# A convolution whose turns run two tiles behind with its middle tap on ScalarE, and expert weights that come as whole gate or up matrices, in one kernel

## The chip, the cores and the metric

The kernel runs on one core of a Trainium2 chip, as one program. A core has five engines that run their own instruction streams and wait for one another by semaphores: TensorE (PE, matrix products; its weight loads are shown apart as PEld), VectorE (DVE), ScalarE (ACT), GpSimd (POOL) and SyncE (SP, which here only issues transfers), and 16 DMA engines that move data between memory and the core. The metric is the device time of one execution in microseconds, lower is better.

## What is computed

The reference chains two blocks of a transformer on 256 tokens of width 1024, each of two layers, all in 32-bit floats. Two places of it matter here. In each layer of the first block a mixture of 32 experts in 4 groups follows the attention: each token goes to one group and to two experts of it.

```python
for g in range(N_GROUPS):
    h = jax.nn.silu(jnp.einsum('td,edf->tef', t, w_gate[g])) * jnp.einsum('td,edf->tef', t, w_up[g])
    y = y + jnp.einsum('tef,efd->td', h * gate[:, g, :, None], w_down[g])
```

Gate and up matrices are 1024 x 256 for each expert, down matrices 256 x 1024. In the second layer of the second block a projection of width 4096 (2048 for x, 1024 each for B and C) goes through a depthwise convolution over the sequence, on 256 tokens of the sequence and 256 of a context:

```python
xbc = jax.nn.silu(dwconv(xbc, conv_w, conv_b))          # 5 taps per channel
xs, bm, cm = jnp.split(xbc, [SSD_DI, SSD_DI + SSD_GN], axis=-1)
```

## The kernel before

**Experts.** Tokens are sorted to experts, 32 places for each; four experts make a quad, whose four products lie side by side in four groups of 32 columns of TensorE. There are eight main quads a layer (all 32 experts) and four overflow quads (8 to 11) for tokens beyond 32, whose experts are chosen at run time. Each quad needs three pieces of weights of 4 MB (f32): k = 0 and k = 1 for gate and up, k = 2 for down. `STEPS_E` sets the order of the quads. The pieces go through a ring of four slots (WQ0, WQ1, W, and a fourth made of a part of XA and of EX); main pieces are issued by SyncE in the order (q, k) at line 480, each as soon as its slot is free (`await_used`), overflow pieces as conditional transfers on ScalarE's queue (`overflow_load`, line 1067). `plan_ring` counts what each slot's semaphore has to reach. Before, pieces 0 and 1 are halves of the rows of K: piece 0 holds K rows 0 to 3 of each partition's eight of both gate and up, piece 1 the other four, and a matmul of `gate_up` (line 731) multiplies 32 columns of tokens with 512 columns, gate beside up. Each such matmul of 32-bit floats shows as two records in the trace: a part has 4 rows of K x 4 experts x 2 = 32. A piece's source is 4 KB in a row for each partition and expert. A down piece has 8 KB in a row. After gate and up VectorE and ScalarE make silu(gate) x up, TensorE turns it (line 554) and `down` multiplies it (line 768).

**Convolution.** The 4096 channels make 32 tiles of 128 channels: m = 0 to 15 (x) and 16 to 23 (B) with 512 columns (sequence and context), called wide here, 24 to 31 (C) with 256, called narrow. For a tile, ScalarE makes the high part PHI of the weights (`conv_high`, line 2784), VectorE the low part WLO (`conv_low`, line 3296), both two tiles ahead; TensorE does 24 matmuls (line 2201) into a bank; ScalarE copies the bank into PRE (`conv_taken`, helper line 2611), which has two padding columns at each side; VectorE adds up five taps into ACC (line 3384 the first, line 3386 the other four); ScalarE applies silu and the bias into XD (`conv_out`, lines 2817 to 2822; ARENA is the memory that holds PRE, ACC and XD); TensorE turns XD to have tokens on partitions ("xt", line 2206), for tiles 0 to 23; and ScalarE copies the turned tile (`conv_turned`). TensorE's order is written out by hand: the matmuls of tile m ("sc", m), then the turn of tile m-1. The eight banks are handed out by the same order. Between the first tiles ScalarE has other work with tables of its own to load (`dt_logs` at m = 2).

## Time and profile before

| | |
|---|---|
| median of 3 runs | 2192.19 us (2192.07 to 2196.28) |
| the profiled execution | 2194.47 us, its span 2192.7 us |
| mean granted clock of TensorE | 0.961 |
| busy: PE, DVE, ACT, POOL | 1977.7, 1256.6, 743.2, 168.1 us |
| moved by DMA | 441.03 MB in 152322 packets, 143856 of them under 8 KB |

The span is from the first to the last instruction of one profiled execution; the device time has a little more around it. The granted clock is the share of full speed that the chip's throttle gave TensorE; its two levels are 1.2 and 2.4 GHz, so that 1.00 in a window is 2.4 GHz throughout and 0.50 is 1.2 GHz. The expert stages lie at 255 to 470 us (layer 0) and 700 to 942 us (layer 1), the convolution at 1605 to 1806 us.

### The profile page before, as it was taken

To read this page: it belongs to the slowest core of one execution; us is meant where nothing else is said; L and a number is where in the kernel's file an instruction comes from. 1 tells how busy PE (TensorE), PEld (TensorE's weight loads), DVE (VectorE), ACT (ScalarE), POOL (GpSimd) and SP (SyncE) were. 2 spreads that over 40 slices of the span, in tenths; PEclk is the share of its full clock that TensorE was granted. 3 is DMA by queue.
4 is the path that set the end of the run, shared out by engine and by line. 5 is a ranking of instruction groups with operands and counts; after the bars stand their busy time and mean duration, and the time that the engine had idled before them with its cause. 6 is when DMAs were issued, how large, how long until landed. Compare 5 with 4: busy or idle time off the path is not lost.

```text
span 2192.7 us, 31068 instructions
## 1 busy us (share of the span) xinstructions
PE 1977.7 (90%) x12070; PEld 1445.9 (66%) x12070; DVE 1256.6 (57%) x2223; ACT 743.2 (34%) x1338; POOL 168.1 (8%) x156
## 2 busy tenths in 40 slices
PE   6989888879899788969998999999979989998997
PEld 4776433337785333337887778888867777777996
DVE  3374522135474212257375776666766887877676
ACT  3363311114552111144233311122164446743332
POOL 2001100010002000034413000000100000000000
PEclk9999999989999999979999999999989999999999
DMA  7479899965699999932212323322222334234552
GB/s 222 168 285 348 322 411 413 413 249 192 224 363 325 362 399 413 413 117 77 77 39 82 130 96 116 105 88 83 80 69 97 118 133 173 77 116 173 192 192 96
DMA packets 152322, 441.03 MB, mean 201 GB/s; under 512 B 10640, under 2 KB 13120, under 8 KB 143856
## 3 DMA queue, kind: packets, MB, share of 16 engines
q1 hardware_dynamic: 143232, 413.77, 50.6%
q0 software_dynamic: 8224, 22.13, 3.3%
q10 hardware_dynamic: 720, 3.15, 0.4%
q8 instruction: 97, 1.59, 0.3%
q14 instruction: 49, 0.40, 0.1%
HBM read 535.31 MB, written 1.21 MB: 245 GB/s over the span
## 4 chain that ended last, share of the span: by engine, by line
PE 39%; DVE 7%; ACT 4%; DVEq 3%; issue 1%; ACTq 0%; DMA 0%; SPq 0%
PE bank L2201 21%; PE bank L2294 12%; PE bank L2345 4%; PE bank L2573 2%; ACT ARENA L2873 1%; DVE ARENA L3386 1%; PE bank L2206 1%; DVEq L3345 1%; DVEq L2971 0%; ACT UT L2634 0%; DVE ARENA L3404 0%; DVEq L3388 0%; ACT ARENA L2611 0%; DVEq L3406 0%; DVE MB L3333 0%
## 5 line engine op out<-in xcount | busy, mean ns | idle before, releaser
L2647 ACT ACTIVATE WPH<-W 128x1024 fp32r<-128x1024 f32 x128 | 135.6, 1064 | 381.1 <-PE bank L2201 200.6
L2201 PE MATMUL bank<-UH,WPH 128*128 128x512 f32 (+1 forms) x512 | 174.6, 341 | 7.2 <-DVE UL L2979 3.1
L2201 PE MATMUL bank<-UL,WPH 128*128 128x512 f32 (+1 forms) x512 | 173.7, 339 | 0.0
L2201 PE MATMUL bank<-UH,WPL 128*128 128x512 f32 (+1 forms) x512 | 173.4, 339 | 0.0
L3017 DVE TENSOR_TENSOR WPL<-W,WPH 128x1024 fp32r<-128x1024 f32 x128 | 153.5, 1220 | 18.6 <-ACT WPH L2647 18.6
L2294 PE MATMUL bank<-WPH,MHH 128*128 128x512 f32 x384 | 149.5, 389 | 0.0
L2294 PE MATMUL bank<-WPL,MHH 128*128 128x512 f32 x384 | 149.5, 389 | 0.0
L2294 PE MATMUL bank<-WPH,MHL 128*128 128x512 f32 x384 | 149.4, 389 | 0.0
L1501 DVE TENSOR_TENSOR H<-SG,bank 128x256 f32<-128x256 f32 x24 | 10.1, 421 | 211.5 <-ACT SG L1073 211.5
L2201 PEld LDWEIGHTS bank<-UH,WPH 128*128 128x128 f32 x512 | 98.4, 192 | 20.0 <-issue 3.8
L2201 PE MATMUL bank<-ARENA 128*128 128x64 f32 (+4 forms) x528 | 102.1, 350 | 6.3 <-issue 2.8
L2201 PEld LDWEIGHTS bank<-UL,WPH 128*128 128x128 f32 x512 | 98.4, 192 | 10.3
L2201 PEld LDWEIGHTS bank<-UH,WPL 128*128 128x128 f32 x512 | 98.4, 192 | 10.2
L2201 PE MATMUL bank<-XHI,PHI 128*128 128x512 f32 (+2 forms) x264 | 101.4, 384 | 4.0 <-DVE XLO L2979 2.4
L2201 PE MATMUL bank<-XHI,WLO 128*128 128x512 f32 (+2 forms) x264 | 98.4, 373 | 0.0
L2201 PE MATMUL bank<-XLO,PHI 128*128 128x512 f32 (+2 forms) x264 | 98.0, 371 | 0.0
L2611 ACT ACTIVATE ARENA<-bank 128x512 f32<-128x512 f32 (+3 forms) x108 | 58.1, 559 | 116.3 <-PE bank L2201 79.2
L731 PE MATMUL bank<-WQ,XG 128*32 128x512 f32 x704 | 83.8, 620 | 14.6 <-DMA WQ<-in_expert_w_up 10.3
L2201 PEld LDWEIGHTS bank<-ARENA 128*128 128x128 f32 (+1 forms) x528 | 77.0, 197 | 26.6 <-issue 22.1
L561 PE MATMUL bank<-W,XT 128*128 128x512 f32 x192 | 88.4, 620 | 6.6 <-ACT XT L912 4.0
L3386 DVE SCALAR_TENSOR_TENSOR ARENA<-ARENA 128x512 f32<-128x512 f32 (+1 forms) x128 | 87.7, 685 | 10.3 <-issue 0.9
L1510 DVE SCALAR_TENSOR_TENSOR EXPERT_ROWS_LOW<-bank,GSLOT,EXPERT_ROWS_HIGH 128x512 fp32r<-128x512 f32 x48 | 34.6, 748 | 94.9 <-ACT EXPERT_ROWS_HIGH L1086 94.9
(482 smaller groups left out, 4412.1 us busy)
## 6 DMA issues: line engine op xcount, KB each, us to landing
W<-in_ffn_w SPq DMA_DIRECT2D x64, 1024.0 KB, 6.6
W<-in_ada_w SPq DMA_DIRECT2D x32, 1024.0 KB, 7.4
WQ<-in_expert_w_gate SPq DMA_DIRECT2D x16, 2048.0 KB
WQ<-in_expert_w_up SPq DMA_DIRECT2D x16, 2048.0 KB
WQ<-in_expert_w_down SPq DMA_DIRECT2D x16, 2048.0 KB
W<-in_w_in SPq DMA_DIRECT2D x24, 1024.0 KB, 7.7
WQ<-in_expert_w_down ACTq DMA_DIRECT2D x24, 1024.0 KB
W<-in_ssd_w_in SPq DMA_DIRECT2D x24, 1024.0 KB, 6.4
```

Of the source, the lines that this page charges most:

```text
L561: last = nc.tensor.matmul(bank[r.bank(key)][:, 0:n], lhs[k], rhs[k], start=(k == 0), stop=(k == len(lhs) - 1))
L731: last = nc.tensor.matmul(bank[r.bank(key)][32 * g:32 * g + 32, :], xg[:, 4 * part + k, col:col + 32], half_of(slot, g, g + 1)[:, 0, :, k, ...
L1510: r.read_done(nc.vector.scalar_tensor_tensor(YL[:, sl], bank[r.bank(key)][:, :], GSLOT[:, q:q + 1], YH[:, sl].bitcast(F32), ALU.mult, ALU. ...
L2201: return nc.tensor.matmul(bank[r.bank(key)][0:rows, cols[0]:cols[1]], lhs, rhs, start=start, stop=stop)
L2206: return nc.tensor.transpose(bank[r.bank(key)][0:m, j * P:j * P + k], src, ident[0:k, 0:k])
L2294: last = nc.tensor.matmul(bank[r.bank(key)][:, :], a, x[:, k, :], start=first and k == 0 and z == 0, stop=last_block and kp == 1 and k == ...
L2345: last = nc.tensor.matmul(bank[r.bank(key)][:, :], x[:, kk, tok], a[:, k, :], start=kp == 0 and k == 0 and z == 0, stop=kp == 3 and k == 1 ...
L2573: last = nc.tensor.matmul(bank[r.bank(key)][:, :], y[:, kk % 2, c0:c0 + P], w[:, k, :], start=kk == 0 and z == 0, stop=kk == 15 and z == 2 ...
L2611: r.read_done(nc.scalar.activation(dst, src, func, **kw), key)
L2647: nc.scalar.activation(piece_view(WPH, q), piece_src(i, q), ACT.Copy).then_inc(hi_done, 1)
L3017: nc.vector.tensor_tensor(piece_view(WPL, q), piece_src(i, q), piece_view(WPH, q).bitcast(F32), ALU.subtract).then_inc(lo_done, 1)
L3386: last = nc.vector.scalar_tensor_tensor(acc, src, CW[:, m, k:k + 1], acc, ALU.mult, ALU.add)
```

## The change

Two parts. In the experts, piece 0 of a quad is now the whole gate matrix of four experts and piece 1 the whole up matrix, 8 KB in a row for each partition and expert; a piece is two transfers of two experts each (one and three in the fourth slot). A matmul multiplies with 256 columns, and there are twice as many. In the convolution, the turn stands two tiles behind the matmuls (`TURN_LAG`), XD has three buffers, the third of which is YI, and ScalarE writes the middle tap straight from the bank into ACC, scaled by a column of weights, so that VectorE has four taps to add and no first one.

```diff
--- before.py
+++ after.py
@@ -55,10 +55,9 @@
     fills = [[] for _ in range(RING)]
     for i in range(3 * MQ):
         q, k = divmod(i, 3)
-        split = 2 if i % RING == RING - 1 else 1
-        fills[i % RING].append(((q, k), 16 * (2 if k == 2 else 2 * split)))
+        fills[i % RING].append(((q, k), 16 * 2))
         if q in OVERFLOW_OF:
-            fills[i % RING].append(((OVERFLOW_OF[q], k), 16 * (4 if k == 2 else 8)))
+            fills[i % RING].append(((OVERFLOW_OF[q], k), 16 * 4))
     at = {}
     for slot, made in enumerate(fills):
         total = 0
@@ -307,8 +306,8 @@
                 return whole[slot][:, g0:g1]
             return first_of_last if g0 == 0 else EX[:, g0 - 1:g1 - 1]
 
-        def half_of(slot, g0, g1):
-            return ring(slot, g0, g1).rearrange("p g (u k f) -> p g u k f", u=2, k=4)
+        def whole_of(slot, g0, g1):
+            return ring(slot, g0, g1).rearrange("p g (k f) -> p g k f", k=KT)
 
         def down_of(slot, g0, g1):
             return ring(slot, g0, g1).rearrange("p g (f n) -> p g f n", f=2)
@@ -382,20 +381,14 @@
         up_w = io["expert_w_up"].rearrange("l g e (p k) f -> (l g e) p k f", p=P)
         down_w = io["expert_w_down"].rearrange("l g e (p k) n -> (l g e) p k n", p=P)
 
-        def piece(slot, what, part, first, g0, g1):
-
-            if what == 2:
-                return down_w[bass.ds(first, g1 - g0)].rearrange("e p k n -> p e k n"), down_of(slot, g0, g1)
-            src = (gate_w, up_w)[part][bass.ds(first, g1 - g0), :, 4 * what:4 * what + 4, :]
-            return src.rearrange("e p k f -> p e k f"), half_of(slot, g0, g1)[:, :, part]
-
-        def parts_of(slot, k):
-
-            if slot == RING - 1:
-                cuts = [(0, 1), (1, 4)]
-            else:
-                cuts = [(0, 2), (2, 4)] if k == 2 else [(0, 4)]
-            return [(part, g0, g1) for part in range(1 if k == 2 else 2) for g0, g1 in cuts]
+        def piece(slot, what, first, g0, g1):
+
+            src = (gate_w, up_w, down_w)[what][bass.ds(first, g1 - g0)].rearrange("e p k n -> p e k n")
+            return src, (down_of if what == 2 else whole_of)(slot, g0, g1)
+
+        def cuts_of(slot):
+
+            return [(0, 1), (1, 4)] if slot == RING - 1 else [(0, 2), (2, 4)]
 
         def await_used(eng, l, key, before):
 
@@ -475,8 +468,8 @@
                     if i == 3:
                         r.filled(sp, ("rout", 1), l)
                     await_used(sp, l, (q, k), True)
-                    for part, g0, g1 in parts_of(i % RING, k):
-                        src, dst = piece(i % RING, k, part, l * NEXP + (4 * q + g0), g0, g1)
+                    for g0, g1 in cuts_of(i % RING):
+                        src, dst = piece(i % RING, k, l * NEXP + (4 * q + g0), g0, g1)
                         sp.dma_start(dst, src).then_inc(landed[i % RING], 16)
             sp.wait_ge(used[2], DEPTH * RING_USES[2] + 1)
             for n, key in enumerate(list(after)[0:SLOTS]):
@@ -725,11 +718,11 @@
                         slot = weights_landed(l, part, q)
                         if part == 0:
                             r.claim(pe, key, l)
-                        for k in range(4):
+                        for k in range(KT):
                             for g in range(4):
                                 col = (q % 2) * P + 32 * g
-                                last = nc.tensor.matmul(bank[r.bank(key)][32 * g:32 * g + 32, :], xg[:, 4 * part + k, col:col + 32],
-                                                        half_of(slot, g, g + 1)[:, 0, :, k, :], start=(part == 0 and k == 0), stop=(part == 1 and k == 3))
+                                last = nc.tensor.matmul(bank[r.bank(key)][32 * g:32 * g + 32, part * EH:(part + 1) * EH], xg[:, k, col:col + 32],
+                                                        whole_of(slot, g, g + 1)[:, 0, k, :], start=(k == 0), stop=(k == KT - 1))
                         if part == 0:
                             last.then_inc(used[slot], 1)
                             if between is not None and q == a:
@@ -1061,10 +1054,9 @@
 
                     slot = PIECE_AT[(q, k)][0]
                     await_used(act, l, (q, k), True)
-                    for part in range(1 if k == 2 else 2):
-                        for g in range(4):
-                            src, dst = piece(slot, k, part, l * NEXP + ids[g], g, g + 1)
-                            nc.scalar.dma_start(dst, src, cond=on[g]).then_inc(landed[slot], 16)
+                    for g in range(4):
+                        src, dst = piece(slot, k, l * NEXP + ids[g], g, g + 1)
+                        nc.scalar.dma_start(dst, src, cond=on[g]).then_inc(landed[slot], 16)
 
                 def silu(q):
 
@@ -1642,6 +1634,7 @@
 NB = 8
 PIECES = 4
 CUM_AT = 8
+TURN_LAG = 2
 TINY = 1e-37
 X_LN = (4, 8, 10, 12)
 SQ_LN = (2, 6, 9, 11)
@@ -1721,13 +1714,12 @@
         r.plan(("uT", "m1", s, j), b)
     keys = [("dt",), ("dtT",)]
     conv = []
-    for m in range(NX + 2 * SG_ + 1):
+    for m in range(NX + 2 * SG_):
         if m == CUM_AT:
             conv += [("cum",), ("cd",)]
-        if m < NX + 2 * SG_:
-            conv.append(("sc", m))
-        if 1 <= m <= NX + SG_:
-            conv.append(("xt", m - 1))
+        conv.append(("sc", m))
+        if TURN_LAG <= m < NX + SG_ + TURN_LAG:
+            conv.append(("xt", m - TURN_LAG))
     keys += conv
     for n, k in enumerate(keys):
         r.plan(k, {("sc", NX + 2 * SG_ - 2): 6, ("sc", NX + 2 * SG_ - 1): 7}.get(k, n % 8))
@@ -1932,7 +1924,7 @@
         o = 18432
         PRE = A_[:, o:o + 1040].rearrange("p (b s n) -> p b s n", b=2, s=2)
         ACC = A_[:, o + 1040:o + 2064].rearrange("p (b s n) -> p b s n", b=2, s=2)
-        XD = A_[:, o + 2064:o + 3088].rearrange("p (b n) -> p b n", b=2)
+        XD = [A_[:, o + 2064:o + 2576], A_[:, o + 2576:o + 3088], YI[:].rearrange("p t n -> p (t n)")]
         CW = A_[:, o + 3088:o + 3280].rearrange("p (m k) -> p m k", k=6)
         SUMS = A_[:, o + 4096:o + 5120].rearrange("p (z j n) -> p z j n", z=2, j=2)
         CVR = A_[0:6, 8192:12288]
@@ -2476,20 +2468,19 @@
                         last = mm(key, (z * SEQ, (z + 1) * SEQ), DA[:, jt, z * 32:z * 32 + 32], SUMS[:, z, jt, :], jt == 0, jt == 1, rows=32)
                 r.fill_done(last, key)
 
-            for m in range(NX + 2 * SG_ + 1):
+            for m in range(NX + 2 * SG_):
                 if m == CUM_AT:
                     sums()
-                if m < NX + 2 * SG_:
-                    key = ("sc", m)
...
-                    r.fill_done(last, key)
+                key = ("sc", m)
...
+                r.fill_done(last, key)
                 if m == 0:
                     key = ("dtT",)
                     r.read(pe, ("dt",))
@@ -2497,12 +2488,13 @@
                     for t in range(4):
                         last = turn(key, t, DTL[:, t * P:(t + 1) * P])
                     r.fill_done(last, key)
-                if 1 <= m <= NX + SG_:
-                    key = ("xt", m - 1)
-                    pe.wait_ge(xd_rdy, m)
+                if TURN_LAG <= m < NX + SG_ + TURN_LAG:
+                    q = m - TURN_LAG
+                    key = ("xt", q)
+                    pe.wait_ge(xd_rdy, q + 1)
                     r.claim(pe, key)
-                    for t in range(4) if m - 1 < NX else range(2, 4):
-                        last = turn(key, t, XD[:, (m - 1) % 2, t * P:(t + 1) * P])
+                    for t in range(4) if q < NX else range(2, 4):
+                        last = turn(key, t, XD[q % 3][:, t * P:(t + 1) * P])
                     r.fill_done(last, key)
 
             def group_pre(g):
@@ -2809,15 +2801,15 @@
             def conv_out(q):
 
                 act.wait_ge(acc_rdy, q + 1)
-                if 2 <= q < NX + SG_:
-                    r.filled(act, ("xt", q - 2))
+                if 3 <= q < NX + SG_:
+                    r.filled(act, ("xt", q - 3))
                 acc = ACC[:, q % 2]
                 bias = CW[:, q, 5:6]
                 if q < NX:
-                    nc.scalar.activation(XD[:, q % 2, :].rearrange("p (s n) -> p s n", s=2), acc, ACT.Silu, bias=bias).then_inc(xd_rdy, 1)
+                    nc.scalar.activation(XD[q % 3].rearrange("p (s n) -> p s n", s=2), acc, ACT.Silu, bias=bias).then_inc(xd_rdy, 1)
                 elif q < NX + SG_:
                     nc.scalar.activation(BDL[:, q - NX, :], acc[:, 0, :], ACT.Silu, bias=bias)
-                    nc.scalar.activation(XD[:, q % 2, SEQ:2 * SEQ], acc[:, 1, :], ACT.Silu, bias=bias).then_inc(xd_rdy, 1)
+                    nc.scalar.activation(XD[q % 3][:, SEQ:2 * SEQ], acc[:, 1, :], ACT.Silu, bias=bias).then_inc(xd_rdy, 1)
                 else:
                     nc.scalar.activation(CDL[:, q - NX - SG_, :], acc[:, 0, :], ACT.Silu, bias=bias).then_inc(xd_rdy, 1)
 
@@ -2827,7 +2819,12 @@
                 ns = 2 if m < NX + SG_ else 1
                 if m >= 2:
                     act.wait_ge(acc_rdy, m - 1)
-                copy(key, PRE[:, m % 2, 0:ns, 2:2 + SEQ], bank[r.bank(key)][:, 0:ns * SEQ].rearrange("p (s n) -> p s n", s=ns))
+                src = bank[r.bank(key)][:, 0:ns * SEQ].rearrange("p (s n) -> p s n", s=ns)
+                r.filled(act, key)
+                nc.scalar.activation(PRE[:, m % 2, 0:ns, 2:2 + SEQ], src, ACT.Copy)
+                if m == 0:
+                    r.read(act, ("cw",))
+                r.read_done(nc.scalar.activation(ACC[:, m % 2, 0:ns], src, ACT.Copy, scale=CW[:, m, SCONV // 2:SCONV // 2 + 1]), key)
 
             def conv_turned(q):
 
@@ -2851,8 +2848,8 @@
                 if m >= 1:
                     conv_out(m - 1)
                 conv_taken(m)
-                if 1 <= m <= NX + SG_:
-                    conv_turned(m - 1)
+                if TURN_LAG <= m < NX + SG_ + TURN_LAG:
+                    conv_turned(m - TURN_LAG)
 
             def segments(g):
 
@@ -3379,13 +3376,11 @@
                     v.wait_ge(xd_rdy, m - 1)
                 acc = ACC[:, m % 2, 0:ns]
                 for k in range(SCONV):
-                    src = PRE[:, m % 2, 0:ns, k:k + SEQ]
-                    if k == 0:
-                        last = nc.vector.tensor_scalar(acc, src, CW[:, m, 0:1], None, ALU.mult)
-                    else:
+                    if k != SCONV // 2:
+                        src = PRE[:, m % 2, 0:ns, k:k + SEQ]
                         last = nc.vector.scalar_tensor_tensor(acc, src, CW[:, m, k:k + 1], acc, ALU.mult, ALU.add)
-                    if k < SCONV - 1:
-                        v.drain()
+                        if k < SCONV - 1:
+                            v.drain()
                 last.then_inc(acc_rdy, 1)
 
             for t in range(2):
```

On SyncE, the first pieces of a layer (after the layer's other loads); 128x4x1024 is partitions x experts x elements in a row. Before:

```order
L480 DMA WQ<-in_expert_w_gate 128x4x1024
L480 DMA WQ<-in_expert_w_up 128x4x1024
L480 DMA WQ<-in_expert_w_gate 128x4x1024
L480 DMA WQ<-in_expert_w_up 128x4x1024
L480 DMA W<-in_expert_w_down 128x2x2048 x2
L480 DMA XA<-in_expert_w_gate 128x1024
L480 DMA EX<-in_expert_w_gate 128x3x1024
L480 DMA XA<-in_expert_w_up 128x1024
L480 DMA EX<-in_expert_w_up 128x3x1024
```

and now:

```order
L473 DMA WQ<-in_expert_w_gate 128x2x2048 x2
L473 DMA WQ<-in_expert_w_up 128x2x2048 x2
L473 DMA W<-in_expert_w_down 128x2x2048 x2
L473 DMA XA<-in_expert_w_gate 128x2048
L473 DMA EX<-in_expert_w_gate 128x3x2048
L473 DMA WQ<-in_expert_w_up 128x2x2048 x2
L473 DMA WQ<-in_expert_w_down 128x2x2048 x2
```

The gate matrix comes first as one piece, and the up matrix as a piece of its own; rows are 2048 elements long, as those of down were, and the fourth slot's piece is two transfers instead of four.

On TensorE, the convolution's first tiles: L2201 are a tile's matmuls (L2193 in the changed kernel), of which the first stands here, and L2206 (L2198) is the turn of a tile, which waits for silu by the semaphore b_conv_out. The wait b_mixer_weights_low is for VectorE's low part. Before:

```order
L2201 MATMUL bank<-XHI,PHI 128x512 [waits b_empty3,b_mixer_weights_low]
...
L2206 MATMUL bank<-ident,ARENA 128x128 [waits b_empty4,b_conv_out]
...
L2201 MATMUL bank<-XHI,PHI 128x512 [waits b_empty5,b_mixer_weights_low]
...
L2206 MATMUL bank<-ident,ARENA 128x128 [waits b_empty6,b_conv_out]
...
L2201 MATMUL bank<-XHI,PHI 128x512 [waits b_empty7,b_mixer_weights_low]
```

and now:

```order
L2193 MATMUL bank<-XHI,PHI 128x512 [waits b_empty3,b_mixer_weights_low]
...
L2193 MATMUL bank<-XHI,PHI 128x512 [waits b_empty4,b_mixer_weights_low]
...
L2198 MATMUL bank<-ident,ARENA 128x128 [waits b_empty5,b_conv_out]
...
L2193 MATMUL bank<-XHI,PHI 128x512 [waits b_empty6,b_mixer_weights_low]
...
L2198 MATMUL bank<-ident,ARENA 128x128 [waits b_empty7,b_conv_out]
...
L2193 MATMUL bank<-XHI,PHI 128x512 [waits b_empty0,b_mixer_weights_low]
...
L2198 MATMUL bank<-ident,YI 128x128 [waits b_empty1,b_conv_out]
```

Two tiles' matmuls now stand ahead of the first turn, and between the silu of a tile and its turn there is always one more tile.

On ScalarE, one wide tile in the middle: L2784 (L2776) the high part for two tiles ahead, L2817 (L2809) silu, L2611 or L2824 the copy of the bank into PRE, L2611 (L2603) of 128x4x128 the copy of the turned tile; b_conv_sum is VectorE's sum of the taps. Before:

```order
L2784 ACTIVATE PHI<-W 128x1024 [waits b_full5]
L2817 ACTIVATE ARENA<-ARENA 128x512 [waits b_full4,b_conv_sum]
L2611 ACTIVATE ARENA<-bank 128x2x256 [waits b_full7,b_conv_sum]
L2611 ACTIVATE ARENA<-bank 128x4x128 [waits b_full0]
L2784 ACTIVATE PHI<-W 128x1024 [waits b_full7]
```

and now:

```order
L2776 ACTIVATE PHI<-W 128x1024 [waits b_full4]
L2809 ACTIVATE YI<-ARENA 128x512 [waits b_conv_sum]
L2824 ACTIVATE ARENA<-bank 128x2x256 [waits b_full6,b_conv_sum]
L2827 ACTIVATE ARENA<-bank,ARENA 128x512
L2603 ACTIVATE ARENA<-bank 128x4x128 [waits b_full7]
L2776 ACTIVATE PHI<-W 128x1024 [waits b_full6]
```

The row of L2827 is added in each tile: the middle tap, from the same bank as the copy above it. On VectorE line 3384, one instruction in each tile, is gone.

## Rows read from the trace of the kernel before

**Rows 1.** Page, part 1: busy time, share of the span, instructions.
```profile
PE 1977.7 (90%) x12070; PEld 1445.9 (66%) x12070; DVE 1256.6 (57%) x2223; ACT 743.2 (34%) x1338; POOL 168.1 (8%) x156
```

**Rows 2.** Windows: us, busy (x) of five engines, PEclk, DMA share, GB/s.
```profile
core 0: us, PE busy (x) PEld busy (x) DVE busy (x) ACT busy (x) POOL busy (x), PEclk, DMA share, GB/s
342.00:353.00 11.00, 9.65 (x88) 2.98 (x83) 4.09 (x9) 2.41 (x5) 0.00 (x0) 1.00 1.02 408
905.00:918.00 13.00, 11.38 (x104) 3.70 (x100) 3.54 (x8) 2.77 (x6) 0.00 (x0) 1.00 1.03 410
391.00:396.00 5.00, 4.72 (x32) 1.15 (x32) 0.00 (x0) 0.00 (x0) 0.00 (x0) 0.68 1.01 421
835.00:839.00 4.00, 4.00 (x28) 1.84 (x24) 0.00 (x0) 0.00 (x0) 0.00 (x0) 1.00 1.02 424
258.00:457.00 199.00, 172.16 (x1346) 75.04 (x1342) 50.40 (x103) 29.42 (x56) 0.00 (x0) 0.97 1.02 413
750.00:760.00 10.00, 9.44 (x76) 2.63 (x72) 2.03 (x5) 1.15 (x3) 0.00 (x0) 0.87 0.94 360
...
463.40:469.40 6.00, 5.97 (x32) 1.61 (x32) 0.75 (x1) 0.69 (x1) 0.00 (x0) 0.51 1.05 387
935.60:941.00 5.40, 5.34 (x32) 1.56 (x32) 0.75 (x1) 0.69 (x1) 0.00 (x0) 0.68 0.81 305
```

**Rows 3.** Timeline, TensorE and its weight loads, expert stages: start, us, [idle before].
```profile
163.81 1.95 PE L656 MATMUL bank<-W,cond 128*32 128x128 f32 x64
...
340.60 3.64 PE L731 MATMUL bank<-W,XG 128*32 128x512 f32 x32
...
340.60 0.16 PEld L731 LDWEIGHTS bank<-W,XG 128*32 128x32 f32 x4 [0.27 <-issue]
...
463.43 1.03 PE L768 MATMUL bank<-XA,H 128*32 128x512 f32 x1 [4.14 <-DMA EX<-in_expert_w_down]
...
935.63 0.59 PE L768 MATMUL bank<-XA,H 128*32 128x512 f32 x1 [2.90 <-DMA EX<-in_expert_w_down]
```

**Rows 4.** Idle time before turns (line 2206); two of them in the timeline.
```profile
  ACT ARENA L2820: 5.0, 3
  ACT ARENA L2817: 4.8, 3
...
1634.07 1.11 PE L2206 MATMUL bank<-ident,ARENA 128*128 128x128 f32 x4 [3.15 <-ACT ARENA L2817]
...
1778.01 0.44 PE L2206 MATMUL bank<-ident,ARENA 128*128 128x128 f32 x2 [2.46 <-ACT ARENA L2820]
```

**Rows 5.** Windows of the convolution, columns as in rows 2.
```profile
1634.80:1641.00 6.20, 6.20 (x18) 4.89 (x17) 5.45 (x10) 2.27 (x3) 0.00 (x0) 0.58 0.00 0
...
1643.50:1679.50 36.00, 36.00 (x172) 28.39 (x171) 23.15 (x30) 13.42 (x20) 0.00 (x0) 0.95 0.34 118
```

**Rows 6.** Timeline of the convolution, VectorE and ScalarE, wide then narrow tiles.
```profile
1632.01 1.23 DVE L3296 TENSOR_TENSOR WLO<-W,PHI 128x1024 fp32r<-128x1024 f32 x1 [3.06 <-ACT PHI L2784]
...
1656.30 3.23 DVE L3386 SCALAR_TENSOR_TENSOR ARENA<-ARENA 128x512 f32<-128x512 f32 x4
...
1785.67 0.51 ACT L2822 ACTIVATE ARENA<-ARENA 128x256 f32<-128x256 f32 x1 [1.91 <-DVE ARENA L3386]
...
1789.32 0.51 ACT L2822 ACTIVATE ARENA<-ARENA 128x256 f32<-128x256 f32 x1 [1.92 <-DVE ARENA L3386]
1789.73 0.37 ACT L2611 ACTIVATE ARENA<-bank 128x256 f32<-128x256 f32 x1
...
1787.11 2.18 DVE L3386 SCALAR_TENSOR_TENSOR ARENA<-ARENA 128x256 f32<-128x256 f32 x4
1789.20 1.22 DVE L3296 TENSOR_TENSOR WLO<-W,PHI 128x1024 fp32r<-128x1024 f32 x1
```

**Rows 7.** Groups of ScalarE from 1160 to 1812 us: xcount, busy, mean ns.
```profile
L2784 ACT ACTIVATE PHI<-W 128x1024 fp32r<-128x1024 f32 x32 | 33.7, 1057 | 0.0
...
L2817 ACT ACTIVATE ARENA<-ARENA 128x512 f32<-128x512 f32 x16 | 11.6, 724 | 31.9 <-DVE ARENA L3386 31.8
...
L2726 ACT ACTIVATE XHO<-bank,ARENA 128x512 fp32r<-128x512 f32 x8 | 4.8, 694 | 0.0
```

More of the change, by code:

```diff
@@ L2477, in sums @@
                 r.fill_done(last, key)
[L2479 removed]
+            for m in range(NX + 2 * SG_):
                 if m == CUM_AT:
                     sums()
[L2482 to L2492 removed]
+                key = ("sc", m)
+                pe.wait_ge(conv_lo, m + 1)
+                hi = PHI[:, m % 3]
+                lo = WLO[:, number[("sc", m // 4)] % SLOTS, :, (m % 4) * P:(m % 4 + 1) * P]
+                width = 512 if m < NX + SG_ else SEQ
+                r.claim(pe, key)
+                for k in range(KT):
+                    for z, (a, x) in enumerate(((hi, XHI), (hi, XLO), (lo, XHI))):
+                        last = mm(key, (0, width), a[:, k, :], x[:, k, 0:width], k == 0 and z == 0, k == KT - 1 and z == 2)
+                r.fill_done(last, key)
                 if m == 0:
```

8 lines of the change are left out of this document (removed).

## The prediction

> **What bounds the kernel now.** I read the page first: TensorE is busy for 90% of the span [rows 1], so what shortens the kernel is TensorE's idle time and its time at a lower clock. Both parts of the change lie in stretches where TensorE stands idle, and those I read by windows and by the timeline.
>
> In the expert stages two things run side by side. From 258 to 457 us TensorE is busy 172.16 of 199 us, while the DMA engines are full and move 413 GB/s [rows 2]. So the weights' arrival sets the pace, and TensorE has 199 − 172 = 27 us to spare in layer 0. That it is the arrival that ends last is seen at each stage's end: the last down-product waits 4.14 us for its weights in layer 0 and 2.90 us in layer 1 [rows 3]. In layer 1 before about 795 us the queue is not full (360 GB/s from 750 to 760 us [rows 2]): the next piece waits there for a free slot, and a faster transfer brings nothing.
>
> In the convolution TensorE sets the pace of wide tiles: 36.0 of 36 us busy for six tiles, so 6.0 us a tile [rows 5]. But its turn of tile m-1 stands right behind the matmuls of tile m and waits for ScalarE's silu of tile m-1: 4.8 us in three waits and 5.0 us in three [rows 4]. The longest is 3.15 us, and behind it the granted clock is 0.58 for 6.2 us [rows 5], that is, part of these at 1.2 GHz.
>
> **The expert part.** The bytes stay. A gate or up piece comes in 8 KB rows instead of 4 KB rows. Stretches in which only gate and up pieces land run at 408 to 410 GB/s (four windows), and stretches in which only down pieces land, which have 8 KB rows already, at 421 to 424 GB/s (four windows); in all of them the DMA share is full [rows 2]. A piece is 4 experts × 1024 × 256 × 4 bytes = 4.194 MB: 10.25 us at 409, 9.93 us at 422.5, so −0.33 us for each piece that lands in a full queue. Layer 0 has 13 of them after 255 us (8 main quads give 16, three come earlier): −4.2. Layer 1 has about 8.5 after 795 us: −2.8. Together −7.0. A bound from the other side is nothing at all (the slower rate of gate and up pieces is then due to something that goes with them other than the row length, as the matmuls that run beside them); the upper bound is all sixteen pieces of each layer plus four overflow pieces' share, −8.8.
>
> The Trainium skill, "DMA: Bandwidth & Descriptors", section "Why small descriptors are slow (HBM only)", has the overhead of a packet fixed at a few cycles beside its beats, by which I estimate from its figures that going from 4 KB to 8 KB would bring about 1.1%, or 0.12 us a piece and 2.5 us in all. The rows have 3.3% between the two kinds, three times as much; I go by the rows.
>
> TensorE pays for that: a part is 64 records of 256 columns instead of 32 of 512. Columns are the same, so the question is what a record costs beside its columns. 32 records of 512 columns on 32-column weights take 3.64 us, 64 records of 128 columns with the same weights' shape take 1.95 us [rows 3]: 107 and 29 ns a record from start to start of the next work, and on the straight line between them a 256-column record takes 55 ns, 64 of them 3.54 us where 32 wide ones took 3.42. That is +0.1 us a part, 24 parts a layer, +2.7 us a layer, under 27 us of spare time [rows 2]: it lies beside the transfers. Its cover is the last wait; it shrinks from 4.14 and 2.90 us to some 2 and 0.5 us (the transfers gain on TensorE there, and the records cost it a little), and stays above nothing. I take +0.3 for the last quad.
>
> Behind those last waits the clock is down: the last down-product has 0.51 and 0.68 granted, and 32 records that take 3.64 us at full clock take 5.97 and 5.34 us [rows 2, 3]. That is 2.3 + 1.7 = 4.0 us. If the shorter wait leaves the clock up, most comes back; a drop followed waits of 2.90 us and more here, and the 2 and 0.5 us that I expect are shorter. I take −3, bounds 0 and −4.
>
> The issue side: SyncE issues a piece as two DMAs of two experts (in slot 3, two instead of four), ScalarE's queue four conditional ones instead of eight for an overflow piece. Nothing is behind these that TensorE waits for, and the queue always has a piece pending in the full stretches: nothing taken. Expert part: −7.0 + 0.3 − 3 = −9.7 (from 0 to −12.8).
>
> **The convolution part.** With the turn two tiles behind, silu of tile m-2 has to be done when the matmuls of tile m are, a whole tile (6.0 us) later than needed before. The longest wait of the turns is 3.15 us, so each has cover of over 2.8 us. The waits that go: 4.8 + 5.0 us less the last, 2.46 us [rows 4], which stands in front of the narrow tiles, where TensorE is not the one that ends last: −7.3. With them goes the low clock after the 3.15 us wait: 6.2 × (1 − 0.58) = −2.6. What could be late next: VectorE's low part, which for one tile waits 3.06 us for ScalarE's high part [rows 6], behind three table loads (bound: that tile's wait stays whole, −3.15 and −2.6 are lost, −5 for the conv part remain); and ScalarE, which gets one more eviction in each tile. A scaled eviction of 512 columns takes 0.69 us, the high part 1.06, silu 0.72 [rows 7]. With all three evictions at that price ScalarE's tile is 3 × 0.69 + 1.06 + 0.72 = 3.9 of 6.0 us: covered by TensorE. VectorE loses its first tap and keeps four of 3.23 us together and the low part of 1.22, 4.5 of 6.0 us [rows 6].
>
> In the eight narrow tiles VectorE and ScalarE set the pace, 3.65 us a tile (silu at 1785.67 and 1789.32 [rows 6]). There the chain closes over ScalarE afterwards: four taps take 2.1 us from start to VectorE's next work (1787.11 to 1789.20), silu starts 0.12 later, the eviction 0.41 after that; it takes 0.37, some 0.3 from start to start, and the second one between 0.37 and 0.69 [rows 6, 7], of which I take 0.45, nearer to the row of the same width; 0.1 to the first tap. 2.1 + 0.12 + 0.41 + 0.3 + 0.45 + 0.1 = 3.45 us or so. 7 × −0.2 = −1.3, and at the end the last tile's second eviction stands ahead of a table load, +0.4: −0.9. With the upper price of the eviction the narrow tiles give nothing.
> Conv part: −7.3 − 2.6 − 0.9 = −10.8 (−5 to −12 where it works).
>
> **Sum.** −9.7 − 10.8 = −20.5 on the profiled execution's 2194.5 us (span 2192.7 and 1.8 around it) = 2174.0; the median of the runs shown is 2.3 lower, 2192.2, which gives 2171.7. As the clock's and the rate's terms lose more on one side than they can win on the other, I say 2173.
>
> **The rivals.**
> *Slower: weight loads that are no longer hidden.* A quartet of loads takes 0.16 us on TensorE's load side [rows 3] and today lies behind 0.43 us of matmuls. With 256 columns the quartets are 16 a part instead of 8, each of 0.22 us. If the loads came in series, a part would take 16 × (0.22 + 0.16) = 6.1 instead of 3.6 us, +2.4, ×24 = +58 us of TensorE time a layer against 27 spare: +31 a layer, +62 in all, with conv −10.8: about 2243. It decides from 27 / 24 = 1.1 us a part on. Against it: 64 records of a quarter of the width took 1.95 us together [rows 3], no 16 × 0.16 on top. 5%. The Trainium skill, "TensorE: Matmul & The Clock Gate", section "The mechanism" (of the part on packing small matmuls), has a weight load overlap the matmuls in flight only where the row group differs; all four here use all 128 rows, so by it this rival would hold. The row of 64 quarter-width records disagrees.
> *The rate does not follow the row length.* Then the conv part alone: 2192.2 − 10.8 = 2181.4. For it: gate and up pieces land beside the matmuls of their own slots, down pieces often in stretches of less engine work. 12%.
> *The wait only moves (conv).* The low part or ScalarE is late in the turn's place: expert part alone, about 2183. 10%.
> *Neither:* 2192. 6%.
> Both as forecast: 67%, with a range of its own of 2166 to 2178.
>
> **How the numbers follow.** A measurement of this kernel tells about 0.2% (4.4 us) from no change. Faster: 67 + 12 + 10 = 89%. Same: 6%, slower: 5%. The range of 8 in 10 reaches down to 2164 (all upper bounds) and up to 2186, past the two cases in which one part works.
>
> **What would show it.** In the profile after: windows with gate and up pieces alone at over 418 GB/s, packets under 8 KB down by at least 33,000 (32 main pieces of 4.194 MB in 4 KB); 64 records of a gate_up part within 3.7 us; last waits under 2.9 us and the granted clock of the last down-product near 1; no wait of a turn for silu over 0.3 us; granted clock 1 behind tile 2; narrow tiles at 3.45 us. The prediction is wrong if a part's 64 records take over 4.7 us, if windows stay at 409, or if VectorE's low part ends TensorE's waits in the convolution.

## The result and the profile after

| kernel | median, us | runs | ratio to the kernel before, 95% |
|---|---|---|---|
| before, beside the changed kernel | 2189.56 (2182.11 to 2196.28) | 12 | |
| changed | 2176.29 (2170.18 to 2184.53) | 12 | 0.9941 [0.9925, 0.9957] |
| changed, once more (x_again) | 2174.24 | 6 | 0.9930 [0.9905, 0.9955] |

The change makes the kernel 13 us (0.6%) faster; 2173 was forecast, from 2192.2. The profiled executions lie further apart, spans of 2192.7 and 2174.6 us, 18 us. Executions of one kernel spread over 14 us here, and the profiled one of before is 5 us above the median of its 12 runs; so a profile's difference of a few microseconds is read below only where other profiles repeat it. Four executions, three of the kernel before and one of t_tap, took 2562 to 8280 us and are left out of the medians below.

The page after: the span, busy time, and the packets.

```profile
span 2174.6 us, 33931 instructions
PE 1973.4 (91%) x13606; PEld 1502.3 (69%) x13606; DVE 1242.7 (57%) x2191; ACT 759.0 (35%) x1370; POOL 168.4 (8%) x156
DMA packets 135404, 441.21 MB, mean 203 GB/s; under 512 B 10352, under 2 KB 12832, under 8 KB 110288
```

TensorE has 1536 more records [rows 1], the narrower matmuls of the experts; packets under 8 KB fell by 33,568, of which 32,768 are the 32 main pieces' (4.194 MB each in rows of 4 KB). The bytes are the same within 0.2 MB.

Windows after, in the columns of [rows 2]: layer 0's full stretch, and the last down-products of both layers.

```profile
258.00:457.00 199.00, 173.81 (x2047) 100.87 (x2048) 50.87 (x105) 29.52 (x57) 0.00 (x0) 0.97 1.01 418
...
459.70:463.40 3.70, 3.64 (x32) 1.13 (x32) 0.75 (x1) 0.69 (x1) 0.00 (x0) 1.00 1.03 350
929.20:934.40 5.20, 5.20 (x32) 1.27 (x32) 0.75 (x1) 0.69 (x1) 0.00 (x0) 0.69 0.84 314
```

The queue moves 418 GB/s over 199 us where it moved 413 [rows 2]. The last down-product of layer 0 runs at the full clock (3.64 us, before 5.97 in its window), that of layer 1 at 0.69 as before (0.68). TensorE's timeline at these places:

```profile
452.27 3.66 PE L724 MATMUL bank<-W,XG 128*32 128x256 f32 x64
...
459.74 0.59 PE L761 MATMUL bank<-XA,H 128*32 128x512 f32 x1 [2.41 <-DMA EX<-in_expert_w_down]
...
929.20 1.03 PE L761 MATMUL bank<-XA,H 128*32 128x512 f32 x1 [3.25 <-DMA EX<-in_expert_w_down]
```

A part of 64 records takes 3.66 us (32 wide ones took 3.64 [rows 3]). The last wait shrank from 4.14 to 2.41 us in layer 0; in layer 1 it did not, 3.25 after 2.90.

The convolution's turns, by the view of line 2198 from 1603 to 1765 us: what TensorE waited for ahead of them, and how often.

```profile
its engine sat idle before it (us, times) until:
  issue: 0.4, 1
```

No turn waits for silu any more, where [rows 4] has 4.8 + 5.0 us. The narrow tiles, ScalarE and VectorE in the timeline:

```profile
1776.90 0.51 ACT L2814 ACTIVATE ARENA<-ARENA 128x256 f32<-128x256 f32 x1 [1.28 <-DVE ARENA L3381]
1777.31 0.37 ACT L2824 ACTIVATE ARENA<-bank 128x256 f32<-128x256 f32 x1
1777.58 0.47 ACT L2827 ACTIVATE ARENA<-bank,ARENA 128x256 f32<-128x256 f32 x1
...
1780.28 0.51 ACT L2814 ACTIVATE ARENA<-ARENA 128x256 f32<-128x256 f32 x1 [1.28 <-DVE ARENA L3381]
...
1776.78 1.22 DVE L3293 TENSOR_TENSOR WLO<-W,PHI 128x1024 fp32r<-128x1024 f32 x1
1778.08 2.17 DVE L3381 SCALAR_TENSOR_TENSOR ARENA<-ARENA 128x256 f32<-128x256 f32 x4
```

A narrow tile takes 3.38 us (1776.90 to 1780.28), before 3.65 [rows 6]; 3.45 was forecast. The second eviction takes 0.47 us and ends at 1778.05, the low part at 1778.00: the two now bound the start of the taps together.

### The profile page after: what moved, and what is told of

It reads as the page before. It is cut to its first block, busy times and chain, and to the rows that moved or that the text cites. A ratio compares the mean times of both kernels' runs of the same rounds, so it can differ in the third digit from the quotient of the medians.

```text
span 2174.6 us, 33931 instructions
## 1 busy us (share of the span) xinstructions
PE 1973.4 (91%) x13606; PEld 1502.3 (69%) x13606; DVE 1242.7 (57%) x2191; ACT 759.0 (35%) x1370; POOL 168.4 (8%) x156
## 3 DMA queue, kind: packets, MB, share of 16 engines
q10 hardware_dynamic: 432, 3.15, 0.3%
## 4 chain that ended last, share of the span: by engine, by line
PE 41%; DVE 7%; ACT 4%; DVEq 3%; issue 1%; ACTq 0%; DMA 0%; SPq 0%
PE bank L2193 23%; PE bank L2286 12%; PE bank L2337 4%; PE bank L2565 2%; ACT ARENA L2870 1%; DVE ARENA L3381 1%; PE bank L2198 1%; DVEq L3342 1%; DVE ARENA L3399 0%; ACT UT L2626 0%; DVEq L3401 0%; ACTq L2629 0%; DVE MB L3330 0%; DMA W<-in_ffn_w 0%; DVE XA L2969 0%
## 5 line engine op out<-in xcount | busy, mean ns | idle before, releaser
L2193 PE MATMUL bank<-UH,WPH 128*128 128x512 f32 (+1 forms) x512 | 174.3, 340 | 8.0 <-DVE UL L2976 3.8
L2193 PE MATMUL bank<-UL,WPH 128*128 128x512 f32 (+1 forms) x512 | 173.2, 338 | 0.0
L2193 PE MATMUL bank<-UH,WPL 128*128 128x512 f32 (+1 forms) x512 | 173.1, 338 | 0.0
L1493 DVE TENSOR_TENSOR H<-SG,bank 128x256 f32<-128x256 f32 x24 | 10.1, 421 | 206.1 <-ACT SG L1065 206.1
L2193 PEld LDWEIGHTS bank<-UH,WPH 128*128 128x128 f32 x512 | 98.2, 192 | 20.5 <-issue 4.5
L2193 PE MATMUL bank<-ARENA 128*128 128x64 f32 (+4 forms) x528 | 103.0, 352 | 6.3 <-issue 2.8
L2193 PEld LDWEIGHTS bank<-UL,WPH 128*128 128x128 f32 x512 | 98.3, 192 | 10.3
L2193 PEld LDWEIGHTS bank<-UH,WPL 128*128 128x128 f32 x512 | 98.1, 192 | 10.2
L2193 PE MATMUL bank<-XHI,PHI 128*128 128x512 f32 (+2 forms) x264 | 100.1, 379 | 4.7 <-DVE XLO L2976 2.4
L2193 PE MATMUL bank<-XHI,WLO 128*128 128x512 f32 (+2 forms) x264 | 97.6, 370 | 0.0
L2193 PE MATMUL bank<-XLO,PHI 128*128 128x512 f32 (+2 forms) x264 | 97.2, 368 | 0.0
L2193 PEld LDWEIGHTS bank<-ARENA 128*128 128x128 f32 (+1 forms) x528 | 77.8, 198 | 26.5 <-issue 21.2
L724 PE MATMUL bank<-WQ,XG 128*32 128x256 f32 x1408 | 83.3, 391 | 11.2 <-DMA WQ<-in_expert_w_up 6.6
L1065 ACT ACTIVATE SG<-bank 128x256 f32<-128x256 f32 x24 | 9.2, 384 | 228.0 <-PE bank L724 125.3
```

Source lines behind the costliest of these rows:

```text
L724: last = nc.tensor.matmul(bank[r.bank(key)][32 * g:32 * g + 32, part * EH:(part + 1) * EH], xg[:, k, col:col + 32], whole_of(slot, g, g + ...
L2193: return nc.tensor.matmul(bank[r.bank(key)][0:rows, cols[0]:cols[1]], lhs, rhs, start=start, stop=stop)
```

## The experiments

Times are medians; the kernel before had 2190.9 us beside the four kernels whose names begin with x, 2190.6 beside those with t and 2190.3 beside those with u. Stretches are read from the timelines: layer 0 and layer 1 from the first gate_up matmul to the end of the last down matmul, the convolution from its first matmul to the first of the next stage.

| profile of | rows, order | layer 0 | layer 1 | its end to the convolution | convolution |
|---|---|---|---|---|---|
| before | 4 KB, old | 218.5 | 228.0 | 663.6 | 201.4 |
| x_conv | 4 KB, old | 217.7 | 224.9 | 663.6 | 186.3 |
| u_conv | 4 KB, old | 218.3 | 226.3 | 663.8 | 188.0 |
| u_cols | 4 KB, old, 256 columns | 218.8 | 227.6 | 661.9 | 186.3 |
| x_rows | 4 KB, new | 218.8 | 229.1 | 663.2 | 186.3 |
| u_rows | 4 KB, new | 219.7 | 228.6 | 663.7 | 188.0 |
| changed | 8 KB, new | 212.9 | 226.0 | 666.8 | 188.0 |
| x_again | 8 KB, new | 212.8 | 223.9 | 663.1 | 187.9 |
| x_exp | 8 KB, new | 214.6 | 225.8 | 666.6 | 197.0 |
| t_lag | 8 KB, new | 212.8 | 226.2 | 666.7 | 189.8 |
| t_tap | 8 KB, new | 215.4 | 225.4 | 666.7 | 194.5 |
| t_busy | 8 KB, new | 214.8 | 223.8 | 665.4 | 188.0 |
| t_cols | 4 KB, old, 256 columns | 218.8 | 240.5 | 662.9 | 188.0 |

**x_conv and u_conv: the convolution part alone.** The kernel before with the changes from TURN_LAG on.

```diff
+TURN_LAG = 2
-        XD = A_[:, o + 2064:o + 3088].rearrange("p (b n) -> p b n", b=2)
+        XD = [A_[:, o + 2064:o + 2576], A_[:, o + 2576:o + 3088], YI[:].rearrange("p t n -> p (t n)")]
...
+                r.read_done(nc.scalar.activation(ACC[:, m % 2, 0:ns], src, ACT.Copy, scale=CW[:, m, SCONV // 2:SCONV // 2 + 1]), key)
```

> The convolution part alone, the experts as before. If the parts are independent: the stretch from the convolution's first matmul to the first matmul of the next stage, 201.4 us before and 188.0 us with both parts, is 188 here too; no turn waits; the narrow tiles are 3.38 us apart; the time is 11 to 13 us below the kernel before. If part of the gain in that stretch is given back later (a lower clock in the stages behind it), the stretch is 188 us but the time is only 6 to 8 us lower. The expert stages (first gate_up matmul to last down matmul, 218.5 us in layer 0 and 228.0 us in layer 1 before) stay within 1.5 us of that; a larger difference is the run-to-run spread of TensorE's clock in the same code.

> The convolution part alone once more, beside the other two: 2176 us as before if 6 runs were enough to know it; if it comes out at 2179 to 2182, the expert part was worth more than the 0 to 2 us that the first comparison gave it.

2176.11 us (0.9934 [0.9912, 0.9955]) and, again, 2176.88 us (0.9935 [0.9909, 0.9960]): 13 to 15 us below the kernel before, beyond the 11 to 13 that were expected. The stretch is 186.3 and 188.0 us, no turn waits. Nothing of it is given back. So the convolution part alone has nearly the whole gain of the change. The two values of the stretch come back in the table, 186.3 or 188.0, and the granted clock tells them apart: ten microseconds from 55 us behind the first matmul, in x_conv and then in u_conv,

```profile
1660.43:1670.43 10.00, 10.00 (x60) 7.97 (x59) 4.14 (x5) 3.16 (x5) 0.00 (x0) 1.00 0.60 210
```

```profile
1658.98:1668.98 10.00, 10.00 (x52) 7.15 (x51) 4.14 (x5) 3.17 (x5) 0.00 (x0) 0.83 0.60 210
```

0.17 of 10 us are the 1.7 us.

**x_exp: the expert part alone.** The kernel before with the changes ahead of TURN_LAG.

```diff
+        def whole_of(slot, g0, g1):
+            return ring(slot, g0, g1).rearrange("p g (k f) -> p g k f", k=KT)
...
+                        for k in range(KT):
```

> The expert part alone, the convolution as before. By the profile of both parts together layer 0 took 212.9 us instead of 218.5 and layer 1 226.0 instead of 228.0: 5.7 + 2.0 = 7.6 us less, and so 5 to 8 us below the kernel before. The rival: what layer 0 gained at its end (2.8 us of full clock in the last down-product) was that one execution's luck, and only the rate remains, 4 to 5 us. The convolution's stretch should be 201 us as before, with the same waits of turns (about 7.3 us before the narrow tiles, the longest 3.2 us).

2187.08 us, ratio 0.9991 [0.9975, 1.0008]: the medians differ by 3.8 us, the interval holds no change at all. Layer 0 came down as expected (214.6 us), layer 1 to 225.8, which is where the three kernels with the old experts lie (224.9 to 228.0). The part is worth less than the two stretches say. It is also a second profile of the convolution of before, whose stretch was expected at 201 us and is 197.0, and there it tells against a term of the forecast. The turn that waits longest, and a window behind it (to be held against [rows 4, 5]):

```profile
1638.62 0.66 PE L2198 MATMUL bank<-ident,ARENA 128*128 128x128 f32 x4 [3.17 <-ACT ARENA L2809]
...
1639.40:1645.40 6.00, 6.00 (x30) 4.90 (x29) 5.42 (x10) 2.65 (x4) 0.00 (x0) 1.00 0.00 0
```

The wait is there as it was, 3.17 us, and the clock behind it is 1.00, not 0.58. The drop in the profile of before was not a fixed price of that wait; t_tap below has a wait of 3.36 us at the same place, and 1.00 in the six microseconds behind it.

**x_again: the changed kernel once more.**

> The changed kernel once more, beside the others on one chip: 11 to 15 us below the kernel before. If the two parts add up, its gain is the sum of the gains of the two parts alone within 3 us; if one hides behind the other or they share clock, it is less by more than that. Its profile shows which of the stages repeat: layer 0 at 213 and layer 1 at 226 us, the convolution at 188 us; a stage that comes out over 2 us away shows how far one execution's clock reaches.

2174.24 us, 0.9930 [0.9905, 0.9955]. The stretches of layer 0 and of the convolution repeat within 0.1 us; layer 1 and what lies behind it come out 2 and 4 us shorter. Gains of the parts alone are 14.7 and 3.8 us, 18.5 together, beside 16.6 here and 13.3 in the first set: the parts add up as far as these sets can tell, with a 3.8 that is not clear of no change by itself.

**x_rows and u_rows: the changed kernel with 4 KB rows.** Only the transfers differ from the changed kernel: halves of K, into the same places.

```diff
-            src = (gate_w, up_w, down_w)[what][bass.ds(first, g1 - g0)].rearrange("e p k n -> p e k n")
-            return src, (down_of if what == 2 else whole_of)(slot, g0, g1)
+            src = (gate_w, up_w)[what][bass.ds(first, g1 - g0), :, 4 * part:4 * part + 4, :]
+            return src.rearrange("e p k f -> p e k f"), whole_of(slot, g0, g1)[:, :, 4 * part:4 * part + 4]
```

> The changed kernel, but each gate or up piece is fetched as two halves of K in 4 KB rows into the same places; pieces, matmuls and their order stay as in the changed kernel. If the row length makes the rate: stretches with gate and up pieces alone fall from 419 to 424 back to 408 to 410 GB/s, the last waits for the down weights grow again to about 4 and 3 us, and the time is 5 to 8 us above the changed kernel. If the rate was due to the order of the pieces or the narrower matmuls, it stays at about 420 and the time within 2 us of the changed kernel.

> The changed kernel with 4 KB rows once more: 2181 us if the row length is worth the 5 to 7 us that the first comparison gave it; within 2 us of the convolution part alone if the difference between them was the spread of the clock between sets of runs.

2181.39 us (0.9960 [0.9946, 0.9974]) and 2183.67 us (0.9967 [0.9952, 0.9981]): 5 to 9 us above the two medians of the changed kernel, neither of which was taken beside u_rows. Layer 0 is back at 218.8 and 219.7 us, and so is the rate. The same window as above, in x_rows, and the last wait:

```profile
258.00:457.00 199.00, 173.18 (x2032) 100.94 (x2034) 50.09 (x103) 29.06 (x55) 0.00 (x0) 0.97 1.02 413
...
463.27 1.03 PE L768 MATMUL bank<-XA,H 128*32 128x512 f32 x1 [3.86 <-DMA EX<-in_expert_w_down]
```

With matmuls and order of the changed kernel the queue moves 413 GB/s again: the rate is the row length's. From the ends of the packets in the trace (packets of 4 KB and more of SyncE's queue counted off in pieces of 4.194 MB, the last sixteen pieces of layer 0), a gate or up piece takes 10.29 us in the kernel before, 10.30 in x_rows, 10.03 in the changed kernel and 10.04 in x_exp. The down pieces between them, with 8 KB rows in all four, take 9.9 to 10.1 us there.

But both sets stand 5 to 7 us above the convolution part alone too, which has the same 4 KB rows. So the new order of the pieces with its narrower matmuls goes with about as much more time as the longer rows bring. That was not foreseen. Part of it can be the clock, whose mean over the executions is 0.9640 and 0.9628 in x_conv and u_conv, 0.9622 and 0.9613 in x_rows and u_rows: by an estimate from these, clock difference times span, at most 3.9 and 3.3 us, which leaves 1.4 and 3.5 us.

**t_cols and u_cols: narrower matmuls alone.** The convolution part with the pieces of before, each matmul made as two; in t_cols gate and up each start their sums in a bank, in u_cols a bank starts once.

```diff
+                        for u in range(2):
...
-                                                        half_of(slot, g, g + 1)[:, 0, :, k, :], start=(part == 0 and k == 0), stop=(part == 1 and k == 3))
+                                                            half_of(slot, g, g + 1)[:, 0, u, k, :], start=(part == 0 and u == 0 and k == 0), stop=(part == 1 and u == 1 and k == 3),
```

> The convolution part with the experts' pieces of before (halves of K of gate and up in 4 KB rows), but each matmul of 512 columns made as one of 256 for gate and one of 256 for up. If narrower matmuls cost what 64 records in 3.66 us instead of 32 in 3.64 say, it is within 2 us of the convolution part alone (2176 us). If they cost more than that in the program (weight loads, instruction fetch), it is 3 us or more above it, which would explain why the changed kernel with 4 KB rows is 5 us above the convolution part alone.

2196.03 us (1.0025 [1.0010, 1.0041]), 20 us above the convolution part. The sums of gate and up are not the reference's in this kernel, so layer 1 routes its tokens otherwise (ScalarE's queue moves 6.29 MB of overflow pieces, in the other kernels 3.15) and takes 240.5 us, 14 more than with the old experts. Only layer 0 can be read: 218.8 us, as with wide matmuls.

> Again the convolution part with the experts' pieces of before, each matmul of 512 columns made as two of 256, now with sums that start once for a bank, so that layer 1 routes as in the reference and the whole time can be read. If the narrower matmuls are what the changed order costs in the experts: about 2181 us, as the changed kernel with 4 KB rows (2181.4), 5 us above the convolution part alone. If narrower matmuls cost nothing beside the transfers: 2176 us, and the 5 us lie in the order of the pieces or in the spread of the clock between sets of runs.

2179.54 us (0.9952 [0.9934, 0.9971]): between the two expectations, 2.7 us above the convolution part measured beside it and 4.1 below u_rows; the intervals of it and of the convolution part overlap. Its mean granted clock, 0.9632, is not below that of u_conv (0.9628). The first two parts of layer 1 together, in u_conv and then in u_cols:

```profile
713.92 7.07 PE L731 MATMUL bank<-WQ,XG 128*32 128x512 f32 x64 [0.94 <-issue]
```

```profile
715.70 7.11 PE L732 MATMUL bank<-WQ,XG 128*32 128x256 f32 x128 [0.94 <-issue]
```

0.02 us a part. If the narrower matmuls cost 2.7 us, it is not in the records themselves.

**t_lag and t_tap: the halves of the convolution part.** In t_tap the turn stands one tile behind (the first edit below); in t_lag VectorE adds five taps again (the second, in part).

```diff
-TURN_LAG = 2
+TURN_LAG = 1
```

```diff
-                    if k != SCONV // 2:
+                    if k == 0:
+                        last = nc.vector.tensor_scalar(acc, src, CW[:, m, 0:1], None, ALU.mult)
+                    else:
```

> The changed kernel, but VectorE adds all five taps again and ScalarE writes no tap: of the convolution part only the turn two tiles behind is left. If the lag alone removes the waits of the turns: no turn waits, the wide tiles take as long as in the changed kernel (about 156 us from the first matmul of the convolution to the first narrow tile), and the narrow tiles go back from 3.38 to 3.65 us, so that the stretch is some 2 us longer than the 188 us of the changed kernel and the time 1 to 3 us above it. If the tap is what matters, turns still wait for silu and the stretch is near 197 us.

> The changed kernel, but the turn stands one tile behind again; ScalarE still writes the middle tap. If the lag is what matters: turns wait again, though less, as VectorE has one operation of 0.5 us fewer ahead of silu and ScalarE one of 0.5 us more; the sum of their waits stays above 5 us and the time is 5 to 9 us above the changed kernel. If the tap alone shortens the chain enough, turns wait under 2 us in sum and the time is within 3 us of the changed kernel.

t_lag: 2175.47 us (0.9926 [0.9905, 0.9947]), no turn waits; two narrow tiles' silu:

```profile
1774.95 0.51 ACT L2814 ACTIVATE ARENA<-ARENA 128x256 f32<-128x256 f32 x1 [1.92 <-DVE ARENA L3378]
...
1778.59 0.51 ACT L2814 ACTIVATE ARENA<-ARENA 128x256 f32<-128x256 f32 x1 [1.90 <-DVE ARENA L3378]
```

3.64 us a narrow tile, and 1.8 us more in the stretch (189.8 us): the tap's share, too small for the times to show. t_tap: 2185.64 us (0.9972 [0.9957, 0.9986]), 9 us above the changed kernel's first median and 10 above t_lag, where 5 to 9 were expected; its stretch is 194.5 us; the turns wait again, the longest as long as ever:

```profile
1636.76 0.66 PE L2198 MATMUL bank<-ident,ARENA 128*128 128x128 f32 x4 [3.36 <-ACT ARENA L2809]
```

The others wait 0.39, 1.23, 0.63, 0.25, 0.71 and 2.49 us. The lag is the part that pays.

**t_busy: TensorE kept busy in the last wait.** Three matmuls whose product is not used, ahead of the last down-product of a layer.

```diff
+                if i == MQ - 1:
+                    r.claim(pe, ("d", i, 0), l)
+                    keep_busy(("d", i, 0), 3)
                 slot = weights_landed(l, 2, i)
```

> The changed kernel with three matmuls of 512 columns, whose product is not used, put into the bank of the last down-product of each layer before TensorE waits for its weights. If TensorE's idle time there is what brings the clock down: the wait of 2.4 to 3.3 us is filled, the last down-product takes 3.6 us in both layers (in layer 1 it took 5.2), and the time is 1 to 2 us below the changed kernel. If the clock falls there for another reason, the down-product stays at 5 us or more in layer 1 and the time is the same or, where the filling runs past the weights' arrival, up to 1 us longer.

2177.01 us (0.9921 [0.9898, 0.9945]), as the changed kernel. The end of layer 1, the turn of the hidden part, the filling and the first and last of the down-product:

```profile
933.89 0.44 PE L547 MATMUL bank<-ident,H 128*128 128x128 f32 x2 [0.96 <-DVE H L1497]
934.90 2.81 PE L671 MATMUL bank<-RC,ident 128*128 128x512 f32 x6 [0.56 <-ACT H L909]
937.64 0.62 PE L765 MATMUL bank<-XA,H 128*32 128x512 f32 x1
...
940.67 0.59 PE L765 MATMUL bank<-XA,H 128*32 128x512 f32 x1
```

The down-product runs through in 3.64 us (937.64 to 941.28), where it took 5.2. In layer 0, where the clock was up in the changed kernel already, the filling ends 3.75 us after the turn's start; in the changed kernel's profile the weights had come after 2.85: 0.9 us lost. From the turn's start to the end layer 1 takes 7.4 us, in the changed kernel 8.9: 1.5 won. Both are below what times can show. So both layers of this one profile have the full clock behind the filling, which fits that TensorE's idle time there brings the clock down. It does not show it, since the clock is up and down without a filling too: 1.00 behind a wait of 2.41 us in layer 0 of the changed kernel, 0.70 behind one of 1.42 us in layer 1 of x_again.

## Why the prediction was right, and where not

The direction and the convolution's mechanism came as forecast, and the time lies in the forecast's range of 2166 to 2178 us. The gain is smaller than forecast, 13 us for 19: the kernel before stands at 2189.6 us over 12 runs, 2.6 below the 2192.2 that the forecast set out from. Inside the sum two errors go against one another: the convolution brought 13 to 15 us instead of 10.8, and the expert part on top of it under 3 instead of 9.7 (the changed kernel's 2176.3 and 2174.2 beside 2176.1 and 2176.9 of the convolution part). That the sum fell so near is luck in part.

**The convolution (−10.8).** Measured −13 to −15 us alone. Waits of turns went as listed, all of them; the lag did that, as t_lag and t_tap show. By the stretch it is 201.4 and 197.0 us in the two profiles with the old convolution against 186.3 to 188.0: −12 on the mean. The waits in front of wide tiles are 7.3 us in both old profiles, and each break seems to cost some tenths more (a turn behind a wait takes 0.66 us in x_exp, 0.60 without a wait in x_conv). The narrow stretch, from the first narrow tile on, gained 1.8 us instead of 0.9: 3.38 us a tile, and the wait of 2.46 us became 1.14. The clock term of −2.6 was read from one profile, and x_exp shows the wait without the drop: a price that comes in some executions only. Over the executions it is there all the same: the mean granted clock is 0.9640 and 0.9628 in the convolution part alone and 0.9615 and 0.9614 in the kernel before beside it, by an estimate from these at most 5.5 and 3.1 us. The rest, 9 to 10 us, are the waits, the breaks and the narrow tiles. What was feared to be late next, the low part behind the table loads, ended no wait ahead of a wide tile.

**The rate of the pieces (−7.0).** −0.33 us a piece was forecast, −0.25 to −0.27 measured, and x_rows shows that it is the row length's. The Trainium skill, "DMA: Bandwidth & Descriptors", section "Why small descriptors are slow (HBM only)", gave an estimate of 1.1% by its fixed overhead of a packet; the pieces show 2.5% (10.29 to 10.03 us), so the rows were the better guide here. The upper bound of the term does not come out of its own figures: 32 pieces at −0.33 are −10.6, not −8.8. In layer 0 the stretch is 4.5 us shorter on the mean of the five profiles with 8 KB (t_busy left out) than of the three with the old experts and wide matmuls, clock included. In layer 1 it is 1 us shorter, where −2.8 for the rate and more for the clock were due.

**The cost of the new order (+0.3).** This is the step that failed: "+0.1 us a part ... under 27 us of spare time ... I take +0.3 for the last quad". The records themselves are cheap, 3.66 us a part. But the changed kernel with 4 KB rows is 5 to 7 us slower than the convolution part with the old experts; in the profiles 1.1 us of it stand in layer 0 and 2.5 in layer 1. Row length and order alone are thus each worth 5 to 9 us and 5 to 7 us, of opposite sign, and little is left. u_cols puts up to 2.7 us on the narrower matmuls, and the granted clock up to 3.9 and 3.3 us on TensorE's speed in the rest of the program; which wait carries the first, and why the clock is lower, is not settled.

**The clock at the ends of the layers (−3).** In layer 0 it came in three of five profiles: where the last wait was 2.29 to 2.41 us (t_lag, x_again and the changed kernel) the down-product took 3.64 us, in t_tap and x_exp, with 2.49 and 3.00 us, it took longer again. In layer 1 the wait of the changed kernel did not shrink (3.25 us) and the clock fell as before. In x_again and t_tap it did shrink there, to 1.42 and 1.22 us, and the clock fell all the same, to 0.70 over the down-product (5.12 and 5.18 us); x_again:

```profile
928.30 1.03 PE L761 MATMUL bank<-XA,H 128*32 128x512 f32 x1 [1.42 <-DMA EX<-in_expert_w_down]
...
928.30:933.40 5.10, 5.10 (x32) 1.29 (x32) 0.75 (x1) 0.69 (x1) 0.00 (x0) 0.70 0.99 372
```

So the length of this wait does not decide it, and the forecast's "if the shorter wait leaves the clock up" did not hold. t_busy fits that idle time has a part in it, and no more. And some of the layers' gain is gone by the convolution: the stretch from layer 1's end to it, in which no instruction was changed, is 661.9 to 663.8 us in all seven profiles with 4 KB rows and 665.4 to 666.8 in five of six with 8 KB. Two windows of it, before and after:

```profile
940.96:1604.54 663.58, 621.45 (x2785) 507.64 (x2785) 448.23 (x665) 192.12 (x262) 99.06 (x63) 0.96 0.25 87
```

```profile
934.40:1601.20 666.80, 624.26 (x2787) 509.41 (x2784) 448.09 (x665) 192.11 (x262) 99.21 (x63) 0.95 0.25 87
```

TensorE has the same matmuls and 2.8 us more of busy time at a granted clock lower by 0.01. Whether the experts' timing decides that or it is the luck of these profiles stays open; x_again has 8 KB rows and 663.1 us.

**The rivals.** Weight loads that are not hidden: no, a part takes 3.66 us and not 6.1. The Trainium skill, "TensorE: Matmul & The Clock Gate", section "The mechanism", by which loads of the same row group would not overlap, is not borne out by this kernel's rows. The case in which the conv part alone works comes nearest to what happened, though not for its reason: the rate does follow the row length, and something else takes it back.

## What to carry to other kernels

A wait of an engine that bounds its stage, for a result of the tile before, goes away with one more tile of lag and one more buffer, and the gain is the sum of these waits and a little more; that is a safer term than any of clock or rate. Where a faster transfer needs a new order of the work, the new order must be timed with the old transfer too: here the two nearly cancelled, and the experts' time alone was not clear of no change. Before a clock drop of one profile is put into a sum, look for a second execution of the same code.

## What was not expected of the hardware

The granted clock after the same wait of 3.15 to 3.17 us was 0.58 in one execution and 1.00 in another, and a down-product behind a wait of 1.42 us had 0.70 where one behind 2.41 us had 1.00. A stretch of 663 us without a changed instruction came out at 661.9 to 666.8 us; in the pair shown, 2.8 of the 3.2 us are TensorE's busy time at the lower clock. Transfers of 8 KB rows moved a 4.194 MB piece in 10.03 us where 4 KB rows took 10.29, at full DMA engines both times.
